# An encoder step on one core: three engines' queues ordered anew in the first mixer's attention, and the next FFN's first weight steps moved into it

## The reference

```python
hp = hp + 0.5 * swiglu(rms_norm(hp, norm_ffn1[l]), ffn1_wg[l], ffn1_wu[l], ffn1_wd[l])
...
# mixer of even layers: HGRN2 recurrence beside selected attention
oa = oa * lax.rsqrt(jnp.mean(oa * oa, axis=-1, keepdims=True) + RMS_EPS)
oa = oa.reshape(B, T, A_VW) * o_gain * jax.nn.sigmoid(ag)
...
s = jnp.einsum('bqhd,bqnd->bqhn', q_b, kg) * (Dh ** -0.5)
s = jnp.where(valid[:, :, None, :], s, NEG_BIG)
p = jax.nn.softmax(s, axis=-1)
ob = jnp.einsum('bqhn,bqnd->bqhd', p, vg)
...
merged = jnp.concatenate([oa, ob.reshape(B, T, B_QW)], axis=-1)
hp = hp + merged @ w_out
hp = hp + 0.5 * swiglu(rms_norm(hp, norm_ffn2[l]), ffn2_wg[l], ffn2_wu[l], ffn2_wd[l])
```

## Time and profile before

| | us |
|---|---|
| median of 3 runs | 2036.16 |
| lowest and highest | 2031.59, 2036.73 |
| the profiled execution, device time | 2029.51 |
| its span, first to last instruction | 2027.7 |
| TensorE busy in it | 1888.8 (93%) |
| VectorE, ScalarE, GpSimd busy | 1379.2, 1222.7, 818.4 |
| mean granted TensorE clock | 0.978 |

### The profile page before, as it was taken

One profiled execution on the slowest core, in us unless ns is written; L12 is line 12 of the kernel. 1 busy time (PEld: TensorE's weight loads), 2 busy tenths in 40 slices (PEclk: granted clock), 3 DMA queues, 4 the chain that ended last, 5 costly groups with the idle time before them and its releaser, 6 DMA issues. The chain is left out here.

```text
span 2027.7 us, 36950 instructions
## 1 busy us (share of the span) xinstructions
PE 1888.8 (93%) x14457; PEld 1433.6 (71%) x14457; DVE 1379.2 (68%) x2155; ACT 1222.7 (60%) x1509; POOL 818.4 (40%) x524
## 2 busy tenths in 40 slices
PE   3899999999989869899999997999999889999999
PEld 2677777776758636577777775777777667777777
DVE  7767873467998652877786348778753697778632
ACT  5677877744933553577787336777853347777631
POOL 6666611111544011376660025766400357666000
PEclk9999999999999879999999999999999989999999
DMA  3222237611201200132322212233232013233330
GB/s 143 84 101 86 104 141 283 226 56 64 73 28 42 100 0 1 43 104 83 105 97 101 94 63 66 101 103 104 99 129 86 21 45 104 87 105 108 114 106 29
DMA packets 29170, 183.96 MB, mean 91 GB/s; under 512 B 3600, under 2 KB 4080, under 8 KB 13440
## 3 DMA queue, kind: packets, MB, share of 16 engines
q1 hardware_dynamic: 22896, 161.08, 22.8%
q0 software_dynamic: 6160, 21.34, 2.9%
HBM read 178.58 MB, written 3.83 MB: 90 GB/s over the span
## 5 line engine op out<-in xcount | busy, mean ns | idle before, releaser
L2347 PE MATMUL ps<-big 128*128 128x296 f16 (+1 forms) x2464 | 714.4, 290 | 29.1 <-DVE big L1495 7.9
L2351 PE MATMUL ps<-big 128*128 128x296 f16 (+1 forms) x2464 | 714.3, 290 | 23.6 <-DVE big L1384 16.8
L2348 PE MATMUL ps<-big 128*128 128x296 f16 (+1 forms) x2464 | 714.2, 290 | 0.0
L2329 PE MATMUL ps<-big 128*128 128x296 f16 (+1 forms) x4296 | 547.0, 289 | 7.8 <-POOL big L550 3.6
L2329 PEld LDWEIGHTS ps<-big 128*128 128x128 f16 x4296 | 414.9, 98 | 131.5 <-DVE big L1503 4.4
L468 POOL TENSOR_TENSOR big<-big 128x512 f32<-128x512 f32 x88 | 118.6, 1348 | 544.9 <-ACT big L733 300.8
L2347 PEld LDWEIGHTS ps<-big 128*128 128x128 f16 x2464 | 242.2, 98 | 107.7 <-ACT ps L778 12.0
L2351 PEld LDWEIGHTS ps<-big 128*128 128x128 f16 x2464 | 242.1, 98 | 99.1 <-DVE big L1384 22.6
L2348 PEld LDWEIGHTS ps<-big 128*128 128x128 f16 x2464 | 242.1, 98 | 65.4 <-issue 0.3
L1495 DVE SCALAR_TENSOR_TENSOR big<-big,scales 128x2048 f16<-128x2048 f32 x88 | 250.8, 2850 | 8.6 <-ACT big L752 7.8
L1490 DVE SCALAR_TENSOR_TENSOR big<-big,scales 128x1536 f16<-128x1536 f32 x88 | 201.8, 2293 | 75.8 <-ACT big L744 75.8
(11 more groups left out here) (351 smaller groups left out, 2655.1 us busy)
## 6 DMA issues: line engine op xcount, KB each, us to landing
big<-in_w_up SPq DMA_DIRECT2D x88, 1024.0 KB, 4.8
big<-in_w_dn SPq DMA_DIRECT2D x32, 1408.0 KB, 6.0
big<-in_w_in POOLq DMA_DIRECT2D x20, 512.0 KB, 6.0
big<-in_w_in SPq DMA_DIRECT2D x20, 512.0 KB, 3.7
big<-in_w_out POOLq DMA_DIRECT2D x8, 512.0 KB, 7.2
big<-in_w_out SPq DMA_DIRECT2D x1, 4096.0 KB, 12.1
resid<-in_x SPq DMA_DIRECT2D x4, 592.0 KB, 6.8
out_y<-resid SPq DMA_DIRECT2D x8, 296.0 KB, 4.7
```

What stands on the lines that cost most here:

```text
L2329: last = mm(ps[:, bank + hf, 0:n], w, x[:, hf * HALF:hf * HALF + n], start=start, stop=stop)
L2347: mm(out, w[:, 0, c], xop[:, 0, x, c, 0:FFN_COLS[f]], start=start, stop=False, skip_group_check=True)
L2348: mm(out, w[:, 1, c], xop[:, 0, x, c, 0:FFN_COLS[f]], start=False, stop=False, skip_group_check=True)
L2351: last = mm(out, w[:, 0, c], xop[:, 1, x, c, 0:FFN_COLS[f]], start=False, stop=(c == DC // 2 - 1), skip_group_check=True)
```

## The change

The work is the same; its order on three queues is new, from the logits of tile 1 to the first products of the FFN. On TensorE the logits of coming tiles are put earlier, up to two tiles ahead of the tile whose chunks are transposed, and the head sums between them; transposes and value products become functions (`turned`, `attended`). On VectorE the masks go ahead of gates, low parts and the probabilities of the tile before; the low parts of output weights come after the last mask. ScalarE's copies and values become `keys_out` and `value_out`. The two `bound`s, scales, high and low parts of the FFN's steps 0 and 1 are spread over the tail of the attention and the output units. Step 2's `bound` goes ahead of the FFN and writes its unused squares to `act_out`. The first four products of stage 2 go P1, P1, P2, P2 where they went P1, P2, P1, P2; the sums and the spread of the second half stay behind the first and second of them.

```diff
 # ScalarE
-            def bound(stage, u, b, width=STEP_W, past_up=False):
+            def bound(stage, u, b, width=STEP_W, past_up=False, scrap=None):
...
-                    out = junk[past_up * (2 if stage == 0 else 1)][:, 0:width]
+                    out = junk[past_up * (2 if stage == 0 else 1)][:, 0:width] if scrap is None else scrap[:, 0:width]
...
-                bound(stage, 2, 0)
+                if stage != 2:
+                    bound(stage, 2, 0)
+                else:
+                    act.wait_ge(rows_done, FFN_UNITS * f + 3)
...
+            exps(0, (0, 1))
+            head_out(3)
+            exps(0, (2, 3))
+            head_out(4)
+            head_square(0)
+            head_square(1)
+            exps(1, (0, 1))
+            head_log(0)
+            keys_out(0, (0,))
+            head_square(2)
+            head_log(1)
+            head_square(3)
+            keys_out(0, (1,))
+            head_log(2)
+            head_log(3)
+            exps(1, (2, 3))
+            for h in range(3):
+                head_root(h)
+            value_out(0)
+            keys_out(1, range(3))
+            exps(2, range(HEADS))
+            head_root(3)
+            value_out(1)
+            keys_out(2, (0, 1))
+            exps(3, (0, 1))
+            head_high(0)
+            head_high(1)
+            keys_out(2, (2, 3))
+            head_high(2)
+            out_high(0)
+            out_high(1)
+            exps(3, (2, 3))
             act.wait_ge(s["out_sem"], 16 * 6)
-            for c in range(5):
-                square_half(1, c, 0)
             bound(2, 0, 0)
+            head_high(3)
+            value_out(2)
+            keys_out(3, (0, 1, 2))
+            out_high(2)
+            bound(2, 1, 1)
+            keys_out(3, (3, 4))
+            out_high(3)
+            square_half(1, 0, 0)
+            exps(4, range(HEADS))
+            out_high(4)
+            value_out(3)
+            keys_out(4, range(5))
+            out_high(5)
+            square_half(1, 1, 0)
+            value_out(4)
+            out_high(6)
+            out_high(7)
+            step_high1(2, 0, 0, False)
+            square_half(1, 2, 0)
+            square_half(1, 3, 0)
+            step_high2(2, 0, 0)
+            square_half(1, 4, 0)
             square_half(1, 5, 0)
-            bound(2, 1, 1)
+            step_high1(2, 1, 1, False)
             square_half(1, 6, 0)
-            step_high1(2, 0, 0, False)
-            step_high2(2, 0, 0)
             square_half(1, 7, 0)
             root_half(2, 0)
-            step_high1(2, 1, 1, False)
+            square_half(1, 0, 1)
+            square_half(1, 1, 1)
             step_high2(2, 1, 1)
-            for c in range(DC):
+            x_highs(1, 0)
+            square_half(1, 2, 1)
+            square_half(1, 3, 1)
+            x_highs(1, 1)
+            square_half(1, 4, 1)
+            bound(2, 2, 0, scrap=act_out.bitcast(F16).rearrange("p b n -> p (b n)"))
+            for c in range(5, DC):
...
 # VectorE
+            def second_half(c):
+
+                out_update(c, 1)
+                if c:
+                    add_half(1, c - 1, 1)
...
             masked(1, range(HEADS))
+            masked(2, (0, 1))
+            probabilities(1)
+            masked(2, (2, 3))
+            head_gate(0)
+            head_gate(1)
+            merged_lows(0)
+            head_gate(2)
+            probabilities(2)
+            head_gate(3)
+            masked(3, (0, 1))
+            probabilities(3, (0,))
+            merged_lows(1)
+            masked(3, (2, 3))
+            masked(4, (0, 1))
+            probabilities(3, (1, 2, 3))
+            masked(4, (2,))
+            merged_lows(2)
+            masked(4, (3,))
+            for u in range(3):
+                out_low(u)
+            out_update(0, 0)
+            out_low(3)
+            out_update(1, 0)
+            weight_scale(2, 0, 0)
+            weight_back(2, 0, 0, inv_x[:, 2:3])
+            probabilities(4)
+            merged_lows(3)
+            out_update(2, 0)
+            out_low(4)
+            dve.wait_ge(sumsq_zero, 2)
+            add_half(1, 0, 0)
+            out_low(5)
+            weight_scale(2, 1, 1)
+            weight_back(2, 1, 1, inv_x[:, 2:3])
+            out_update(3, 0)
+            add_half(1, 1, 0)
+            merged_lows(4)
+            add_half(1, 2, 0)
+            out_low(6)
+            out_low(7)
+            out_update(4, 0)
+            add_half(1, 3, 0)
+            step_low1(2, 0, 0)
+            out_update(5, 0)
+            add_half(1, 4, 0)
+            step_low2(2, 0, 0)
+            out_update(6, 0)
+            add_half(1, 5, 0)
+            out_update(7, 0)
+            add_half(1, 6, 0)
+            second_half(0)
+            add_half(1, 7, 0)
+            step_low1(2, 1, 1)
+            out_update(1, 1)
+            norm_half(2, 0)
+            out_update(2, 1)
+            add_half(1, 0, 1)
+
+            def updates_between():
+
+                add_half(1, 1, 1)
+                out_update(3, 1)
+
+            x_first(2, updates_between)
+            add_half(1, 2, 1)
+            out_update(4, 1)
+            add_half(1, 3, 1)
+            step_low2(2, 1, 1)
+            for c in range(5, DC):
+                second_half(c)
...
 # TensorE
-                order = [(0, "P1"), (0, "P2"), (1, "P1"), (1, "P2")] if halves else \
+                order = [(0, "P1"), (0, "P2"), (1, "P1"), (1, "P2")] if stage in (3, 5) else \
                     [(0, "P1"), (1, "P1"), (0, "P2"), (1, "P2")]
...
+            logits(1, (0, 1))
+            head_sums(0)
+            logits(1, (2,))
+            turned(0, (0,))
+            logits(1, (3,))
+            logits(2, (0,))
+            head_sums(1)
+            turned(0, (1,))
+            head_sums(2)
+            logits(2, (1,))
+            head_sums(3)
+            logits(2, (2, 3))
+            attended(0)
+            logits(3, (0,))
+            turned(1, range(3))
+            logits(3, (1,))
+            attended(1)
+            turned(2, range(4))
+            logits(3, (2, 3))
+            logits(4, (0, 1))
+            attended(2)
+            logits(4, (2, 3))
+            turned(3, (0, 1, 2))
+            pe.wait_ge(s["oa_low"], HEADS)
+            pe.wait_ge(s["pv_low"], 3)
+            out_unit(0, 0)
+            turned(3, (3, 4))
+            out_unit(1, 0)
+            for b in range(2):
+                unit_total(2, b, b)
+            attended(3)
+            out_unit(2, 0)
+            turned(4, range(5))
+            attended(4)
+            for u in range(3, OUT_UNITS):
+                out_unit(u, 0)
+            pe.wait_ge(s["pv_low"], TILES)
+            for u in range(OUT_UNITS):
+                out_unit(u, 1)
+                if u in (1, 2):
+                    (sums_half if u == 1 else spread_half)(2, 0)
```

More of the change, by code:

```diff
@@ L1257, in _, with value_out @@
                     last.then_inc(s["pt_evac"], 1)
[L1258 to L1272 removed]
+            def value_out(t):
                 act.wait_ge(s["pv_mm"], t + 1)
@@ L2129, in merged_lows, with probabilities @@
                 last.then_inc(s["pv_low"], 1)
-            def probabilities(t):
+            def probabilities(t, heads=range(HEADS)):
                 r, w, x = ROWS[t], WIDTH[t], t % 2
-                for h in range(HEADS):
+                for h in heads:
                     dve.wait_ge(s["exp_done"], t * HEADS + h + 1)
@@ L2145, in masked @@
                     if h == 0 and t >= 2:
-                        dve.wait_ge(s["pt_mm"], sum(len(key_chunks(i)) for i in range(t - 1)))
+                        dve.wait_ge(s["pt_mm"], chunks_until(t - 1))
                     bank = 2 * (h % 2)
@@ L2818, in logits, with turned @@
                     last.then_inc(s["logit_mm"], 1)
-            ev = 0
-            head(0)
-            pe.wait_ge(s["state_done"], 2)
-            exchange_head(3)
-            head(1)
-            merged_sum()
-            pe.wait_ge(s["state_done"], 4)
-            exchange_head(4)
-            head(2)
-            logits(0, (0, 1))
-            head(3)
-            logits(0, (2, 3))
-            head(4)
-            for t in range(TILES):
-                r = ROWS[t]
-                if t + 1 < TILES:
-                    logits(t + 1, (0, 1))
-                if t == 0:
-                    head_sums(0)
-                for kw, kc, parts in key_chunks(t):
+            def turned(t, chunks):
+                r = ROWS[t]
+                for c in chunks:
+                    kw, kc, parts = key_chunks(t)[c]
+                    ev = chunks_until(t) + c
                     if ev == 0:
@@ L2884, in _ @@
                 last.then_inc(s["pv_mm"], 1)
-                if t == 3:
-                    out_unit(2, 0)
-            pe.wait_ge(s["masked_done"], TILES * HEADS)
-            pe.wait_ge(s["pt_evac"], ev)
-            for u in range(4, OUT_UNITS):
+            head(0)
+            pe.wait_ge(s["state_done"], 2)
+            exchange_head(3)
```

(13 more changed lines are left out.)

116 lines of the change are left out of this document (10 added, 106 removed).

## The result

The changed kernel took 1999.44 us (median of 4 runs, 1997.72 to 2004.99), the kernel before on the same chip 2033.88 us (4 runs, 2029.61 to 2036.73): ratio 0.9837 (95% interval 0.9808 to 0.9866), 34.4 us less. The forecast was 2001 us, and 35 us less. The profiled execution took 1998.06 us with a span of 1996.2 us.

The account below looks back on a forecast made before the run. Bound taken: the attention's round trip between engines, not any one engine. Gains 36.6 + 1.4 + 1.9 = 39.9 us, less 2 and about 3, taken as 35: from median 2036.16 to 2001 us, range 1991 to 2018.

Parts of the forecast that it names:

- What bounds: Attention and output projection: the round trip logits, mask, exp, multiply, transpose, copy binds; 29.7 us idle, 14.6 us lower clock.
- The walk: Three new queues followed with old trace durations from 694.83 us: out_unit(0) at 739.1, sums asked at 781.5, resumed at 802.6.
- the 5 us set against it: Allowance on the walk's gain: 2 us for a slow-clock stretch and about 3 us of further short waits.
- The lead at the second sums: TensorE reaches the second half of the sums at 802.6 instead of 839.22: 36.6 us, 24.9 idle and 11.7 clock.
- Weight steps: First FFN bounds, scales, high and low parts move to 732 to 795 us, hidden by output units; 2.85 us wait goes.
- Mixing beside out_low: GpSimd's mixing of steps 0 and 1 at about 736 to 748, beside out_low and probabilities(4), with 3 us cover.
- Into the FFN: Second sums to first FFN products: 8.0 us instead of 9.5, gaining 1.4; moving bound(2, 2, 0) removes a 1.88 us gap.
- The raw sum of 39.9: Whole gain before allowances: 36.6 up to the second sums, plus 1.4 and 1.9 into the FFN.
- A: Rival: the clock stays low through the fp32 part because of the kind of work; gain 21, time 2015; chance 0.21.
- B: Rival: contention makes VectorE late by up to 5.1 us; gain 30, time 2006; counted within the forecast's 0.70.
- C: Rival: masks and multiplies come no sooner, low parts of output weights stand behind; +9.4 us, time 2045.6; chance 0.03.
- D: Rival: nothing changes, idle time moves to other waits of the same round trip, within 0.3% (6 us); chance 0.03.

Follow-up runs that it names:

- filled: Kernel before, with unread fp32 products of 512 columns put into four of TensorE's idle times: 2032.76 us, ratio 0.9988 to the kernel before.
- steps_behind: Changed kernel with the weight steps of FFN steps 0 and 1 back behind the attention: 2006.48 us, ratio 0.9854 to the kernel before.
- late_logits: Changed kernel with only TensorE's queue altered, each tile's logits at most one tile ahead: 2018.66 us, ratio 0.9928 to the kernel before.

## Why the prediction was right

*What bounds.* Right: idle time fell by 21.5 us (29.7 to 8.2) with the same work on all engines, and 12.5 us of it came back when TensorE's lookahead alone was taken away.

*The walk.* Taken from the stage's start, the trace follows it: attended(1) at 21.7 us (in the walk 716.7 - 694.83 = 21.9), out_unit(0) at 45.05 (44.3), first sums at 89.0 (86.7), second at 110.0 (107.8). Of the waits that I named, that ahead of logits(3, 0) is 1.54 us (1.25), that for masked(3, 2) 0.57 (0.4), that for out_update(3) 0.71 (0.75); the 1.1 us ahead of turned(2) did not come. Two were missed: 1.30 ahead of logits(4, 0), and 1.56 ahead of out_unit(0). The walk was 2.2 us early in all, less than the 5 us set against it. On the span's own clock these places lie 5.35 us later still, which no step of the walk holds.

*The lead at the second sums*, 36.6 raw, measured 34.4. Its split into 24.9 of idle time and 11.7 of clock measured 21.5 and 12.8, but the split is only bookkeeping. `filled` shows that the clock's share was not to be had by the clock itself. In the new order, where TensorE hardly waits, a fall of the clock does cost (3.5 us between two profiles of the same program).

*Weight steps.* Right that they are hidden: the first sums do not wait. Mis-sized in what they are worth, some 6 us by `steps_behind` and not the 2.85 us of the first sums alone: the walk had not priced that the old places also hold up the second sums.

*Mixing beside out_low.* "Which have 3 us cover" failed: out_low slowed to 1.84 us each, and of out_unit(0)'s wait 0.84 us is due to it. In the last adds the price was inside the bounds. VectorE in order of time:

```profile
778.12 2.34 DVE L1520 SCALAR_TENSOR_TENSOR big<-big,scales 128x2048 f16<-128x2048 f32 x1
...
799.88 0.66 DVE L1480 TENSOR_TENSOR square_sum<-square_sum,work 128x296 f32<-128x296 f32 x1
800.47 3.39 DVE L1520 SCALAR_TENSOR_TENSOR big<-big,scales 128x2048 f16<-128x2048 f32 x1
804.22 1.10 DVE L1480 TENSOR_TENSOR square_sum<-square_sum,work 128x296 f32<-128x296 f32 x1
```

0.66 and 1.10 us an add against 0.47 alone, 3.39 for the low part against 2.34, and 0.23 us of it reach the sums (0.4 forecast).

*Into the FFN.* 7.81 us measured, 8.0 forecast; the bound's term 1.6, forecast 1.9. The sizes held, a reason did not: "P1 of step 1 now hides root and diagonal" is not what shortens the way to P5, since it stays 7.80 us with the old product order. With the weight steps behind the attention it is 8.55, so about half of the 1.65 us is theirs; the rest I did not take apart.

The raw sum of 39.9 met 37.6 us in the stage, and the 35 taken met 34.4 between medians. That the last two agree to 0.6 us is partly luck: the two profiled executions differ by only 31.5 us, the later start of the stage is in no step of mine, and another profile of the same program has a stage 3.5 us longer.

*The rivals.* A fell by `filled`, and by the fp32 part of the new kernel itself (0.90 from the start of the stage to 739 us). Its price was worked out too low: at a mean clock of 0.75, 45 us of full-speed work take 60, +15 and not +11, which puts A at about 2019 instead of 2015, just outside the range that was meant to hold it. B's price is real but about 1 us on the path (0.84 and 0.23). C and D did not occur.

Open is what VectorE's and ScalarE's new order is worth alone, since `late_logits` breaks it too, and why the stage starts later in all profiles of the new kernels.

## What to carry to other kernels

When several engines are each half idle in one stage and wait for each other in turn, count the round trip and put the next tiles' first operations into the in-order queues far enough ahead; walk all queues together, since one engine's lookahead helps only if the others' order expects it. Don't price a low clock by itself in a stage bound by waits: raised there without the waits going, it gave nothing, and it cost once they were gone. Look at where the next wait stands before taking a small one away: of the waits of 1.5 us and less one only moved, one came back in part, and where two together gave way by 1.7 us the time showed nothing.

## What was not expected of the hardware

TensorE's clock in one stretch of the same program differed between profiles (0.83 against 0.94 in 31 us), worth 3.5 us, although nothing in the queues differs. Idle-time products raised the mean clock of the stage's first 56.5 us from 0.75 to 0.83 and gave no time. A VectorE multiply-subtract of 128x1024 took 1.26 us alone and 1.84 beside GpSimd's mixing, 46% more.
